# The first output projection of a two-block network in three rounded passes: weights split by ScalarE and GpSimd, outputs head by head

## The chip, the cores and the metric

The kernel runs on one core of a Trainium2 chip. The metric is the device time of one execution in microseconds, as the median over runs. TensorE multiplies (PE in the profile), VectorE (DVE), ScalarE (ACT) and GpSimd (POOL) work on whole tiles, and SyncE (SP) issues the weight loads in one queue. Each engine runs its own instructions in order; between engines the order is kept by semaphores.

## What is computed

Two blocks follow each other. The change lies in the first: 512 tokens (256 of context, 256 latent) of width 1024 pass through a gated linear attention with four heads, each scanned in both directions. The outputs of the heads are normalised, multiplied by a gate and projected.

```python
def gla_mixer(h_ctx, h_lat, w_in, a_w1, a_w2, a_b, norm_g, w_out, with_ctx_out):
    proj = h @ w_in
    q, k, v, r = jnp.split(proj, ...)      # 4 heads: q, k of 128, v of 256 each
    for d in range(2):
        g = jax.nn.log_sigmoid((h @ a_w1[d]) @ a_w2[d] + a_b[d]) / GLA_GATE_NORM
        ...                                # scan of each head, both directions summed
    # rms_norm of the head's output, times silu(r), then  @ w_out   (1024 x 1024)

x = x + g1 * o
x = x + g2 * conv_ffn(modulate(x, norm2_g, sh2, s2), ...)
```

Behind it stand the feed-forward block, a neighbourhood attention with a second feed-forward block, and the second network: a long convolution, a second scan and 64 experts.

## The kernel before

**Products.** A float32 product (`mm` on float32 tiles) leaves two records on TensorE. Many projections of the kernel are done otherwise, in three passes over rounded operands: `split_mm` (lines 537 to 541) multiplies the rounded weights by the rounded input (line 539), the rounded weights by the input's rest (540), and the weights' rest by the rounded input (541). The rounded part is a copy into a tile of the rounded float type (ScalarE, `activation` with Copy, helper `A`, line 1273), the rest is the difference, written in place (VectorE, `w_rest`, line 1837, `h_rest`, line 1842).

**Weights.** All weights of the first network come as slabs of 2 MB, one after the other through SP's queue (line 421), into four ring places of 4096 columns. `first_block_slabs` writes out the place of each and the semaphore value that frees it. The late modulation rows (`ada_w`, 20 slabs) use the places 0, 1 and 2, the two slabs of this projection (`gla_w_out`) the places 2 and 0. The first feed-forward slab follows in place 1, free after the last modulation product, the second in place 3, free once the last head's gated output (which lives there as `g_r`) is transposed.

**The scan** goes over eight (head, direction) pairs `hd`, here called heads 0 to 7 of the scan; each two of them make one output head. For each of them TensorE runs `scan_scores`, `scan_keys`, `gate_logits(hd + 2)`, `scan_updates` in two parts, with `late_turn` and, for odd ones from 3 on, `y_turn` (transposes of an output head, line 740) between, then `late_rows` (products of modulation rows, line 593) and for odd ones `scan_out` (lines 727 and 731). VectorE runs `decayed(hd + 1)` (lines 1979 and 1981, which wait for ScalarE's exponentials), `mask_scores`, `gated` for even ones, `states` (lines 2015 and 2018) and `cumulate(hd + 2)` (up to line 1969). ScalarE runs `keys_turned`, `late_read`, `gate_log(hd + 2)`, `y_turned` for odd ones from 3 on (it writes the transposed output with its gain into `g_qk`), `decays(hd + 2)` (seven exponentials) and `scan_norm` for odd ones. GpSimd has two multiplications in each (line 469).

**The projection** makes eight outputs `m` of 128 x 512, each from eight products `k`; `k` = 6 and 7 need the last output head. The first five outputs run ahead over `k` = 0 to 5 (line 765), with `late_turn(7)` after output 0 and `y_turn(3)` after output 2. Then the loop over `m` finishes them and makes the other three (line 777). After output `m`, `residual_norm` issues the norm product of output `m - 1` (line 524), which waits for ScalarE's square, which waits for VectorE's residual (line 1821). ScalarE and VectorE split the first two half slabs of the feed-forward block before the first of these residuals. When all squares are summed, the norm's factor, the modulation and `ffn(0, ...)` follow.

Of the kernel before, what the change touches and what calls it, by code (L numbers as in the profile page):

```python
# [83 lines left out]
def first_block_slabs():  # L84
# [23 lines left out]
    def ffn(l):  # L108
        for j in range(FC // 2):
            add("ffn_w_in", l, j, DC, 512, ("ffn_in_mm", 44 * l + 4 * j + 4), slot(), ("gla_y_tr", HEADS) if l == 0 and j == 1 else None)  # L110
        for m in range(DC):
            add("ffn_w_out", l, m, FC, P, ("ffn_out_mm", 8 * l + m + 1), slot())
# [13 lines left out]
def build(nc, d, out):  # L126
    ctx = ExitStack()
    with ctx:
# [85 lines left out]
        ada_late_sb = carve(g_aw1_at)(3, P)  # L214
        g_r = ring[3][:, :].rearrange("p (t n) -> p t n", n=D)
        g_kdt = kg[:, 0:4 * P].rearrange("p (a b) -> p a b", b=P)

# [101 lines left out]
        def slot(n):  # L319
            return ring[n][:, :]  # L320
# [138 lines left out]
        def _(pool):  # L459
# [5 lines left out]
            for hd in range(8):  # L465
                h, p = hd // 2, hd % 2
                for i, (x, y) in enumerate(((g_e3[:, two(h, p), :], g_qk[:, h, :]), (g_tm[:, p, :], g_qk[:, 4 + h, :]))):
                    pool.wait_ge(S["decay"], 7 * hd + 5 + i)
                    pool.tensor_tensor(x, x, y, ALU.mult).then_inc(S["late_decayed"], 1)

            pool.wait_ge(S["ffn_out_mm"], DC)
# [40 lines left out]
        def _(pe):  # L512
# [230 lines left out]
            for hd in range(8):  # L743
                scan_scores(hd)
                scan_keys(hd)
                if hd == 0:
                    pe.wait_ge(S["gla_r_ev"], 8)
                if hd + 2 < 8:
                    gate_logits(hd + 2)
                scan_updates(hd, 0)  # L750
                if hd >= 1:
                    late_turn(hd - 1)
                else:
                    late_rows(hd, 0)
                if hd >= 3 and hd % 2:
                    y_turn(hd // 2 - 1)
                scan_updates(hd, 1)
                for i in range(0 if hd else 1, ADA_BATCH[hd]):
                    late_rows(hd, i)
                if hd % 2:  # L760
                    scan_out(hd // 2)
            for m in range(GLA_AHEAD):
                w = got(FIRST["gla_out"] + m // 4)
                for k in range(6):
                    mm(pb[m][:, :], w[:, k, 128 * (m % 4):128 * (m % 4) + 128], g_qk[:, 4 * (k % 2) + k // 2, :], start=k == 0, stop=False,  # L765
                       skip_group_check=True)
                if m == 0:
                    late_turn(7)
                if m == 2:
                    y_turn(HEADS - 1)  # L770
            pe.wait_ge(S["gla_y_ev"], 2 * HEADS)
            for m in range(DC):
                w = got(FIRST["gla_out"] + m // 4)
                if m >= GLA_AHEAD:
                    pe.wait_ge(S["proj_x"], 2 * (m - GLA_AHEAD + 1))
                for k in range(6 if m < GLA_AHEAD else 0, DC):
                    last = mm(pb[m % GLA_AHEAD][:, :], w[:, k, 128 * (m % 4):128 * (m % 4) + 128], g_qk[:, 4 * (k % 2) + k // 2, :], start=k == 0, stop=k == DC - 1,  # L777
                              skip_group_check=True)
                last.then_inc(S["proj_mm"], 1)
                residual_norm("n2_0", m, TT)  # L780
# [32 lines left out]
            def na_out(j):  # L813
                pe.wait_ge(S["na_pt"], 2 * j + 2)
                if j >= 2:
                    pe.wait_ge(S["na_o_ev"], j - 1)
                for k in range(4):
# [35 lines left out]
            na_out(NA_H - 1)  # L853
            pe.wait_ge(S["na_o_ev"], NA_H)
            project("na_out", lambda k: n_o[:, k, :], NT, 2 * DC, 1, "n2_1")
# [403 lines left out]
        def _(act):  # L1259
# [236 lines left out]
            def y_turned(h):  # L1496
                act.wait_ge(S["gla_y_tr"], h + 1)
                for e in range(2):
                    A(g_qk[:, 4 * e + h, :], pb[6 + e][:, :], ACT.Copy, scale=col("gng", e)).then_inc(S["gla_y_ev"], 1)

            def r_read(s):
                for u in range(4):
# [10 lines left out]
            for hd in range(8):  # L1513
# [7 lines left out]
                if hd + 2 < 8:  # L1521
                    decays(hd + 2)
                if hd % 2:
                    scan_norm(hd // 2)
            late_read(7)
            y_turned(HEADS - 1)
            act.wait_ge(S["ada_late"], 8)
            for i in range(2):
                ffn_w_in_hi(0, i)
            squares("n2_0", DC, lambda c: xT[:, c, :], ("proj_x", 0, 2))  # L1530
            root_factor("n2_0", DC, 7, TT)
# [255 lines left out]
        def _(dve):  # L1787
# [233 lines left out]
            def gated(h):  # L2021
                dve.wait_ge(S["gla_r_ev"], 8)
                dve.wait_ge(S["o_ev"], 6 * h + 6)
                for tt in range(4):
                    y, o = g_r[:, tt, 256 * h:256 * h + 256], 256 * (tt % 2)
                    STT(out=y, in0=pb[6 + tt // 2][:, o:o + 256], scalar=g_n[:, 4 * (h % 2) + tt:4 * (h % 2) + tt + 1], in1=y, op0=ALU.mult, op1=ALU.mult)\
                        .then_inc(S["gate_y"], 1)

            def sine_argument(i):

# [19 lines left out]
            for hd in range(8):  # L2050
# [6 lines left out]
                if hd + 2 < 8:  # L2057
                    cumulate(hd + 2)
            late_columns(7)
            gated(HEADS - 1)  # L2060
            dve.wait_ge(S["ada_late"], 8)
            ada_gain(0, 1)
            for w in range(2):
                last = ada_gain(1, w)
            last.then_inc(S["mod_ready"], 1)
            for i in range(2):
                ffn_w_in_lo(0, i)
            for m in range(DC):
                residual(m, "proj_mm", "proj_x", m % GLA_AHEAD, TT, 0, 2)
            norm_mod("n2_0", 1, TT)  # L2070
            ffn(0, TT)
# [583 lines left out]
```

## Time and profile before

| | |
|---|---|
| median of three runs | 2468.7 us (2468.6 to 2469.37) |
| the profiled execution | 2463.28 us |
| its span | 2461.5 us |
| granted TensorE clock, mean | 0.919 |
| busy: PE, DVE, ACT, POOL | 2011.6, 909.3, 659.1, 58.4 us |
| TensorE on the chain that ended last | 52% of the span |
| transfers on that chain | 28% of the span |

The page gives each engine's busy time and divides the span into 40 slices with the busy share of each engine in tenths, the clock that TensorE was granted and what the transfers moved. The chain of waits goes back from the last instruction to what released it, step by step. The groups of instructions carry a line number; a line can be a helper's, as 1273 is for all of ScalarE's activations. The timeline lists one engine's instructions in order of time, runs of equal ones merged, with the idle time before them in brackets and the engine that ended it.

### The profile page before, as it was taken

Reading aid. Unit: us, or ns where it says so; the run is one execution under the profiler, and the core shown is the slowest. Engines: PE = TensorE matmul, PEld = TensorE weight load, DVE = VectorE, ACT = ScalarE, POOL = GpSimd, SP = SyncE. Lnnn points to the kernel's source line nnn. Section 1 sums busy time; section 2 is a strip of 40 time slices with the busy share of each in tenths; the row PEclk is TensorE's granted clock in tenths of the full one; section 3 lists DMA queues with packets and bytes.
Section 4 is the critical chain, followed back from the end, with each engine's and each line's share of the span. In section 5 each row is a group of like instructions: output and inputs, shape, how many; then the busy total and the mean of one; then the engine's idle time right before and its main releaser. Section 6 shows DMA issues by size and latency. Waiting matters only on the chain.

```text
span 2461.5 us, 37332 instructions
## 1 busy us (share of the span) xinstructions
PE 2011.6 (82%) x16358; PEld 1478.3 (60%) x16358; DVE 909.3 (37%) x1620; ACT 659.1 (27%) x1143; POOL 58.4 (2%) x83
## 2 busy tenths in 40 slices
PE   6998898999998998999999997766656666666665
PEld 3896555888776885899898454443333333333332
DVE  2345623434523328466475453322211111111112
ACT  4233414323413326454444301111111111111111
POOL 0010100000000001000010000000000000000000
PEclk8998999999999999999999998888888888888888
DMA  8106841222223231343540153999999999999996
GB/s 330 69 35 249 367 172 69 103 103 82 71 92 125 103 117 47 137 174 140 192 174 9 42 221 137 428 426 427 427 427 427 426 427 427 427 428 426 427 428 292
DMA packets 44544, 592.60 MB, mean 241 GB/s; under 512 B 5549, under 2 KB 5737, under 8 KB 8288
## 3 DMA queue, kind: packets, MB, share of 16 engines
q1 hardware_dynamic: 40608, 579.36, 57.5%
q0 software_dynamic: 2992, 8.96, 1.1%
q8 instruction: 130, 2.13, 0.4%
q10 hardware_dynamic: 784, 1.91, 0.2%
q14 instruction: 30, 0.25, 0.0%
HBM read 589.16 MB, written 1.05 MB: 240 GB/s over the span
## 4 chain that ended last, share of the span: by engine, by line
PE 52%; DMA 28%; DVE 6%; ACT 3%; issue 2%; SPq 0%; DVEq 0%; ACTq 0%
DMA s_ring<-in_w_up 12%; PE bank L539 10%; PE bank L541 10%; PE bank L540 10%; DMA s_arena<-in_w_up 8%; PE bank L1152 5%; DMA s_xT<-in_w_up 4%; DMA s_hT<-in_w_up 3%; PE bank L1166 2%; PE bank L593 1%; PE bank L777 1%; PE bank L582 1%; PE bank L1139 1%; DMA s_ring<-in_slabs 1%; PE bank L765 1%
## 5 line engine op out<-in xcount | busy, mean ns | idle before, releaser
L539 PE MATMUL bank<-s_arena_r 128*128 128x256 f32 (+2 forms) x1656 | 549.6, 332 | 39.3 <-DVE s_hT_r L1842 33.5
L1273 ACT ACTIVATE s_arena<-bank 32x256 f32<-32x256 f32 (+7 forms) x439 | 174.0, 409 | 1079.5 <-PE bank L1152 572.1
L541 PE MATMUL bank<-s_arena_r,s_ring_r 128*128 128x512 f32 (+2 forms) x1312 | 443.9, 338 | 0.0
L1152 PE MATMUL bank<-s_ring,s_arena 128*32 128x256 f32 x2048 | 297.6, 507 | 144.4 <-DMA s_xT<-in_w_up 47.4
L540 PE MATMUL bank<-s_hT_r,s_arena_r 128*128 128x512 f32 (+2 forms) x1096 | 369.8, 337 | 0.0
L539 PEld LDWEIGHTS bank<-s_arena_r 128*128 128x128 f32 x1656 | 315.3, 190 | 79.6 <-issue 37.9
L1837 DVE TENSOR_TENSOR s_ring_r<-s_ring,s_arena_r 128x2048 fp32r<-128x2048 f32 (+1 forms) x96 | 232.4, 2425 | 289.6 <-ACT s_arena_r L1273 289.5
L1152 PEld LDWEIGHTS bank<-s_ring,s_arena 128*32 128x32 f32 x2048 | 145.1, 144 | 220.9 <-issue 207.5
L541 PEld LDWEIGHTS bank<-s_arena_r,s_ring_r 128*128 128x128 f32 x1312 | 252.2, 192 | 27.2
L1273 ACT ACTIVATE s_arena_r<-s_ring 128x2048 fp32r<-128x2048 f32 (+1 forms) x96 | 193.2, 2016 | 138.1 <-PE bank L541 137.3
L2420 DVE TENSOR_TENSOR s_arena<-s_arena,bank 64x256 f32<-64x256 f32 x64 | 27.1, 423 | 543.9 <-ACT s_arena L1273 543.9
L540 PEld LDWEIGHTS bank<-s_hT_r,s_arena_r 128*128 128x128 f32 x1096 | 211.1, 193 | 21.8
L1152 PE MATMUL bank<-s_arena 128*32 128x256 f32 x1024 | 121.0, 489 | 75.5 <-DMA s_arena<-in_w_up 32.3
L1152 PEld LDWEIGHTS bank<-s_arena 128*32 128x32 f32 x1024 | 62.5, 139 | 113.3 <-issue 105.2
L540 PE MATMUL bank<-s_ring_r,s_arena_r 128*128 128x256 f32 (+1 forms) x464 | 130.1, 280 | 0.0
L1273 ACT ACTIVATE s_arena<-s_arena 128x512 f32<-128x512 f32 (+8 forms) x172 | 85.4, 532 | 160.6 <-DVE s_arena L1830 83.6
L1152 PE MATMUL bank<-s_xT,s_arena 128*32 128x256 f32 x512 | 92.8, 542 | 38.7 <-DMA s_ring<-in_w_up 38.7
L540 PE MATMUL bank<-s_arena_r 128*128 128x512 f32 (+1 forms) x352 | 120.0, 341 | 0.0
L2476 DVE COPY s_arena<-bank 32x256 f32<-32x256 f32 x128 | 54.3, 424 | 143.4 <-PE bank L1166 141.0
L1152 PE MATMUL bank<-s_hT,s_arena 128*32 128x256 f32 x512 | 82.2, 492 | 17.5 <-DMA s_ring<-in_w_up 17.5
L541 PE MATMUL bank<-s_arena_r,s_hT_r 128*128 128x256 f32 (+1 forms) x336 | 94.3, 281 | 0.0
L540 PEld LDWEIGHTS bank<-s_ring_r,s_arena_r 128*128 128x128 f32 (+1 forms) x464 | 85.9, 185 | 0.5
(332 smaller groups left out, 2621.9 us busy)
## 6 DMA issues: line engine op xcount, KB each, us to landing
s_ring<-in_slabs SPq DMA_DIRECT2D x72, 2048.0 KB, 8.2
s_ring<-in_w_down SPq DMA_DIRECT2D x32, 2048.0 KB, 28.9
s_ring<-in_w_up SPq DMA_DIRECT2D x32, 2048.0 KB, 32.9
s_ring<-in_w_gate SPq DMA_DIRECT2D x32, 2048.0 KB, 33.4
s_arena<-in_w_gate SPq DMA_DIRECT2D x16, 2048.0 KB, 33.5
s_arena<-in_w_up SPq DMA_DIRECT2D x16, 2048.0 KB, 34.0
s_arena<-in_w_down SPq DMA_DIRECT2D x16, 2048.0 KB, 28.9
s_ring<-in_slabs SPq DMA_DIRECT2D x16, 1408.0 KB, 6.4
```

The source lines that it names most:

```text
L539: mm(out, w_hi_, x_hi_, start=start, stop=False)
L540: mm(out, w_hi_, x_lo_, start=False, stop=False)
L541: return mm(out, w_lo_, x_hi_, start=False, stop=stop)
L582: last = mm(pb[m % 4][:, 0:T], w[:, c, 128 * (m % 4):128 * (m % 4) + 128], src(c), start=c == 0, stop=c == DC - 1)
L593: last = mm(bank[32 * j:32 * j + 32, o:o + P], ada_sc[:, c, :], w[:, c, P * j:P * j + P], start=c == 0, stop=c == DC - 1, skip_group_check ...
L765: mm(pb[m][:, :], w[:, k, 128 * (m % 4):128 * (m % 4) + 128], g_qk[:, 4 * (k % 2) + k // 2, :], start=k == 0, stop=False, skip_group_check ...
L1152: last = mm(pb[b][32 * q:32 * q + 32, 0:256], x[:, c, :], w[q // 2][:, c, 256 * (q % 2):256 * (q % 2) + 256], start=c == 0, stop=c == DC - ...
L1166: last = mm(pb[3 + b][32 * q:32 * q + 32, 0:256], e_hT[:, b, 64 * a + 32 * half_:64 * a + 32 * half_ + 32], w[:, 2 * half_ + a, 256 * q:25 ...
L1273: return act.activation(out, in_, func, **kw)
L1837: TTn(view_r, view, hi.bitcast(F32), ALU.subtract).then_inc(S["w_lo"], 1)
L2420: return TTn(e_hid[0:64, b, :], e_sg[0:64, b, :], pb[b][64:128, 0:256], ALU.mult)
L2476: dve.tensor_copy(y_g[32 * j:32 * j + 32, g % 2, 256 * q:256 * q + 256], pb[3 + b][32 * q:32 * q + 32, 0:256]).then_inc(S["y_dve"], 1)
```

## The change

The products of the projection are done by `split_mm`. Their rounded weights (`g_wo_hi`) take the place of the ring's place 1 for outputs 0 to 3 and of the scan's states `g_S` for outputs 4 to 7. ScalarE makes them in four halves (`wo_rounded`): two in the scan's last step, once the last modulation product is done, two behind `late_read(7)`. GpSimd subtracts them from the weights in place. The gated output of each head is rounded by ScalarE (`y_hi`, into the place of that head's values `g_v`) and its rest formed by VectorE (`y_rest`, in place): heads 0 and 1 in the steps 4 and 6 of the scan, behind `decays` and `cumulate`, head 2 at its end, head 3 behind its gain. A wait on each `k` replaces the one wait for the last head. The first feed-forward slab is free only after four outputs, and its two splits move behind the squares and residuals of outputs 3 and 4. The semaphore `na_o_ev` gets an offset for its later users, `rope_s`, `gla_r_ev` and `late_decayed` are counted on.

```diff
@@ first_block_slabs: ffn
-            add("ffn_w_in", ..., slot(), ("gla_y_tr", HEADS) if l == 0 and j == 1 else None)
+            add("ffn_w_in", ..., slot(), {0: ("proj_mm", 4), 1: ("gla_y_tr", HEADS)}.get(j) if l == 0 else None)
@@ tiles
+        g_y_lo = arena_r[:, 0:8 * TT].rearrange("p (a b) -> p a b", b=TT)
+        g_y_hi = arena_r[:, 8 * TT:8 * TT + 4 * D].rearrange("p (t n) -> p t n", n=D)
+        g_wo_hi = [x.rearrange("p (c n) -> p c n", n=512) for x in (ring_r[1][:, :], arena_r[:, g_S_at:g_S_at + 4096])]
+        A_YO_HI, A_WO_HI, A_WO_LO, A_YO_LO = 8, 8, 16, 8
@@ GpSimd, behind the scan's multiplications
+            for q in range(4):
+                n = FIRST["gla_out"] + q // 2
+                pool.wait_ge(S["gla_r_ev"], A_WO_HI + q + 1)
+                pool.tensor_tensor(half(place_r[n], q % 2), half(place[n], q % 2), half(g_wo_hi[q // 2], q % 2).bitcast(F32), ALU.subtract)\
+                    .then_inc(S["late_decayed"], 1)
@@ TensorE
+            def gla_out(m, first, last_k):
+                wh, wl, o = g_wo_hi[m // 4], place_r[FIRST["gla_out"] + m // 4], 128 * (m % 4)
+                if m % 2 == 0:
+                    pe.wait_ge(S["late_decayed"], A_WO_LO + m // 2 + 1)
+                for k in range(first, last_k):
+                    h, e = k // 2, k % 2
+                    pe.wait_ge(S["rope_s"], A_YO_LO + k + 1)
+                    last = split_mm(pb[m % GLA_AHEAD][:, :], wh[:, k, o:o + 128], wl[:, k, o:o + 128], g_y_hi[:, :, 256 * h + P * e:256 * h + P * e + P],
+                                    g_y_lo[:, 4 * e + h, :], k == 0, k == DC - 1)
+                return last
             for m in range(GLA_AHEAD):
-                w = got(FIRST["gla_out"] + m // 4)
-                for k in range(6):
-                    mm(pb[m][:, :], w[:, k, ...], g_qk[:, 4 * (k % 2) + k // 2, :], start=k == 0, stop=False, skip_group_check=True)
+                gla_out(m, 0, 6)
...
-            pe.wait_ge(S["gla_y_ev"], 2 * HEADS)
             for m in range(DC):
-                w = got(FIRST["gla_out"] + m // 4)
                 if m >= GLA_AHEAD:
                     pe.wait_ge(S["proj_x"], 2 * (m - GLA_AHEAD + 1))
-                for k in range(6 if m < GLA_AHEAD else 0, DC):
-                    last = mm(...)
-                last.then_inc(S["proj_mm"], 1)
+                gla_out(m, 6 if m < GLA_AHEAD else 0, DC).then_inc(S["proj_mm"], 1)
                 residual_norm("n2_0", m, TT)
@@ ScalarE
+            def y_hi(h):
+                act.wait_ge(S["gla_y_ev"], 2 * h + 2)
+                for e in range(2):
+                    o = 256 * h + P * e
+                    A(g_y_hi[:, :, o:o + P], g_qk[:, 4 * e + h, :].rearrange("p (t n) -> p t n", n=P), ACT.Copy).then_inc(S["na_o_ev"], 1)
+
+            def wo_rounded(q):
+                n = FIRST["gla_out"] + q // 2
+                act.wait_ge(S[landed[n][0]], landed[n][1])
+                if q == 0:
+                    act.wait_ge(S["ada_mm"], 2 * ADA_N)
+                if q == 2:
+                    act.wait_ge(S["o_mm"], HEADS)
+                A(half(g_wo_hi[q // 2], q % 2), half(place[n], q % 2), ACT.Copy).then_inc(S["gla_r_ev"], 1)
@@ ScalarE, the scan's loop
                 if hd + 2 < 8:
                     decays(hd + 2)
+                if hd in (4, 6):
+                    y_hi(hd // 2 - 2)
+                if hd == 7:
+                    y_hi(2)
+                    for q in range(2):
+                        wo_rounded(q)
                 if hd % 2:
                     scan_norm(hd // 2)
             late_read(7)
+            for q in range(2, 4):
+                wo_rounded(q)
             y_turned(HEADS - 1)
+            y_hi(HEADS - 1)
             act.wait_ge(S["ada_late"], 8)
-            for i in range(2):
-                ffn_w_in_hi(0, i)
-            squares("n2_0", DC, lambda c: xT[:, c, :], ("proj_x", 0, 2))
+            for c in range(DC):
+                square(norms["n2_0"][0], c, xT[:, c, :], ("proj_x", 0, 2))
+                if c in (3, 4):
+                    ffn_w_in_hi(0, c - 3)
@@ VectorE
+            def y_rest(h):
+                for e in range(2):
+                    o = 256 * h + P * e
+                    dve.wait_ge(S["na_o_ev"], 2 * h + e + 1)
+                    TTn(g_y_lo[:, 4 * e + h, :]..., g_qk[:, 4 * e + h, :]..., g_y_hi[:, :, o:o + P].bitcast(F32), ALU.subtract).then_inc(S["rope_s"], 1)
@@ VectorE, the scan's loop
                 states(hd)
                 if hd + 2 < 8:
                     cumulate(hd + 2)
+                if hd in (4, 6):
+                    y_rest(hd // 2 - 2)
+            y_rest(2)
             late_columns(7)
             gated(HEADS - 1)
+            y_rest(HEADS - 1)
...
-            for i in range(2):
-                ffn_w_in_lo(0, i)
             for m in range(DC):
                 residual(m, "proj_mm", "proj_x", m % GLA_AHEAD, TT, 0, 2)
+                if m in (3, 4):
+                    ffn_w_in_lo(0, m - 3)
```

## Rows read from the trace of the kernel before

**Rows 1.** Page, 40 slices of the span: busy tenths of TensorE, GB/s moved

```profile
PE   6998898999998998999999997766656666666665
...
GB/s 330 69 35 249 367 172 69 103 103 82 71 92 125 103 117 47 137 174 140 192 174 9 42 221 137 428 426 427 427 427 427 426 427 427 427 428 426 427 428 292
```

**Rows 2.** Chain of waits, scan's head 5 and projection: start us, us, what

```profile
282.92 11.81 DMA s_ring<-in_slabs
...
294.77 1.95 PE bank L593 x64
...
387.75 6.88 PE bank L777 x16
```

**Rows 3.** Lines 765 and 777, TensorE: count, duration ns min/median/max, first and last start

```profile
L765 PE MATMUL bank<-s_arena,s_ring x60: 592/592/697, 333.0 to 359.5; 128*128 128x512 f32 x60
...
L777 PE MATMUL bank<-s_arena,s_ring x68: 592/592/592, 359.9 to 394.0; 128*128 128x512 f32 x68
```

**Rows 4.** Timeline, TensorE, 345 to 440: start us, us, line, count, [idle before]

```profile
359.95 3.60 PE L777 MATMUL bank<-s_arena,s_ring 128*128 128x512 f32 x8
...
396.25 1.13 PE L524 MATMUL bank<-s_sq,s_ones 128*128 128x512 f32 x2 [0.77 <-ACT s_sq L1273]
404.72 0.76 PE L539 MATMUL bank<-s_arena_r 128*128 128x512 f32 x1 [7.35 <-DVE s_hT_r L1842]
...
406.14 0.63 PE L539 MATMUL bank<-s_arena_r 128*128 128x512 f32 x1
...
407.42 0.63 PE L539 MATMUL bank<-s_arena_r 128*128 128x512 f32 x1
```

**Rows 5.** Line 539, TensorE, 413 to 439.9 us, columns as in rows 3

```profile
L539 PE MATMUL bank<-s_arena_r x39: 389/397/398, 412.8 to 439.4; 128*128 128x512 f32 x39
```

**Rows 6.** Timeline, TensorE, end of the scan

```profile
291.44 1.13 PE L717 MATMUL bank<-s_arena 64*128 64x256 f32 x6 [0.79 <-DVE s_arena L2018]
...
310.36 5.37 PE L593 MATMUL bank<-s_ring,s_arena 128*32 128x128 f32 x128
...
322.80 3.70 PE L593 MATMUL bank<-s_ring,s_arena 128*32 128x128 f32 x128
```

**Rows 7.** Timelines of ScalarE and VectorE, one split each; line 469, GpSimd

```profile
411.68 1.90 ACT L1273 ACTIVATE s_arena_r<-s_ring 128x2048 fp32r<-128x2048 f32 x1
...
413.61 2.29 DVE L1837 TENSOR_TENSOR s_ring_r<-s_ring,s_arena_r 128x2048 fp32r<-128x2048 f32 x1 [1.03 <-ACT s_arena_r L1273]
...
L469 POOL TENSOR_TENSOR s_arena<-s_arena x16: 1264/1399/1863, 165.9 to 304.1; 128x512 f32<-128x512 f32 x16
```

**Rows 8.** Line 421, slab loads: 366 to 372 us, then 0 to 12 us

```profile
L421 SPq DMA_DIRECT2D s_ring<-in_slabs x1: 328/328/328, 368.9 to 368.9; - x1
...
DMA to landing us min/median/max: 7.9/7.9/7.9
...
L421 SPq DMA_DIRECT2D s_ring<-in_slabs x4: 417/541/762, 1.2 to 2.9; - x4
...
DMA to landing us min/median/max: 13.7/22.0/29.8
```

**Rows 9.** Timelines of VectorE and ScalarE, one residual and one square

```profile
363.58 0.88 DVE L1821 SCALAR_TENSOR_TENSOR s_xT<-bank,s_mod,s_xT 128x256 f32<-128x256 f32 x2 [0.84 <-PE bank L777]
...
364.49 0.63 ACT L1273 ACTIVATE s_sq<-s_xT 128x512 f32<-128x512 f32 x1 [1.09 <-DVE s_xT L1821]
```

**Rows 10.** Two stretches: us, each engine's busy time, granted clock, DMA share, GB/s

```profile
310.00:315.00 5.00, 5.00 (x112) 4.66 (x113) 1.45 (x3) 0.00 (x0) 0.00 (x0) 0.66 0.19 39
405.00:410.00 5.00, 5.00 (x13) 3.89 (x13) 2.48 (x5) 5.00 (x11) 0.00 (x0) 0.52 0.02 3
```

**Rows 11.** Timelines of ScalarE and VectorE, heads 4 and 5 of the scan

```profile
284.72 2.91 ACT L1273 ACTIVATE s_arena<-s_arena 128x512 f32<-128x512 f32 x7 [9.32 <-DVE s_arena L1969]
...
285.38 1.29 DVE L1981 TENSOR_TENSOR s_arena<-s_arena 128x512 f32<-128x512 f32 x2 [0.69 <-ACT s_arena L1273]
...
289.87 1.51 DVE L2018 SCALAR_TENSOR_TENSOR s_arena<-s_arena,bank 128x256 f32<-128x256 f32 x3
```

More of the change, by code:

```diff
@@ L109, in ffn @@
         for j in range(FC // 2):
-            add("ffn_w_in", l, j, DC, 512, ("ffn_in_mm", 44 * l + 4 * j + 4), slot(), ("gla_y_tr", HEADS) if l == 0 and j == 1 else None)
+            add("ffn_w_in", l, j, DC, 512, ("ffn_in_mm", 44 * l + 4 * j + 4), slot(), {0: ("proj_mm", 4), 1: ("gla_y_tr", HEADS)}.get(j) if l == 0 else None)
         for m in range(DC):
@@ L761, in _ @@
                     scan_out(hd // 2)
+            def gla_out(m, first, last_k):
[8 more added lines that the diff above has]
+                return last
             for m in range(GLA_AHEAD):
-                w = got(FIRST["gla_out"] + m // 4)
-                for k in range(6):
-                    mm(pb[m][:, :], w[:, k, 128 * (m % 4):128 * (m % 4) + 128], g_qk[:, 4 * (k % 2) + k // 2, :], start=k == 0, stop=False,
-                       skip_group_check=True)
+                gla_out(m, 0, 6)
                 if m == 0:
@@ L770, in _ @@
                     y_turn(HEADS - 1)
-            pe.wait_ge(S["gla_y_ev"], 2 * HEADS)
             for m in range(DC):
-                w = got(FIRST["gla_out"] + m // 4)
                 if m >= GLA_AHEAD:
                     pe.wait_ge(S["proj_x"], 2 * (m - GLA_AHEAD + 1))
-                for k in range(6 if m < GLA_AHEAD else 0, DC):
-                    last = mm(pb[m % GLA_AHEAD][:, :], w[:, k, 128 * (m % 4):128 * (m % 4) + 128], g_qk[:, 4 * (k % 2) + k // 2, :], start=k == 0, stop=k == DC - 1,
-                              skip_group_check=True)
-                last.then_inc(S["proj_mm"], 1)
+                gla_out(m, 6 if m < GLA_AHEAD else 0, DC).then_inc(S["proj_mm"], 1)
                 residual_norm("n2_0", m, TT)
@@ L815, in na_out @@
                 if j >= 2:
-                    pe.wait_ge(S["na_o_ev"], j - 1)
+                    pe.wait_ge(S["na_o_ev"], A_YO_HI + j - 1)
                 for k in range(4):
@@ L853, in _ @@
             na_out(NA_H - 1)
-            pe.wait_ge(S["na_o_ev"], NA_H)
+            pe.wait_ge(S["na_o_ev"], A_YO_HI + NA_H)
             project("na_out", lambda k: n_o[:, k, :], NT, 2 * DC, 1, "n2_1")
@@ L2027, in gated @@
                         .then_inc(S["gate_y"], 1)
+            def y_rest(h):
+                for e in range(2):
+                    o = 256 * h + P * e
+                    dve.wait_ge(S["na_o_ev"], 2 * h + e + 1)
+                    TTn(g_y_lo[:, 4 * e + h, :].rearrange("p (t n) -> p t n", n=P), g_qk[:, 4 * e + h, :].rearrange("p (t n) -> p t n", n=P),
+                        g_y_hi[:, :, o:o + P].bitcast(F32), ALU.subtract).then_inc(S["rope_s"], 1)
             def sine_argument(i):
```

## The prediction

> **What bounds the kernel now.** I read the page's slices first: TensorE is busy for nine or more tenths of most of the first half, and only then do transfers set the pace [rows 1]. The output projection lies between 333 and 396 us, so what the engines before the expert loads lose or gain there reaches the end one for one. The chain of waits comes next [rows 2]. It has two pieces that matter: in the scan's head 5 it runs over a weight transfer of the late modulation rows that lands at 294.73 us, with TensorE there only just before it, and over the projection it runs along TensorE's own products. Of the 71.7 us from the first product at 333.0 [rows 3] to the first product of the feed-forward block at 404.72 [rows 4] the products take 64 x 0.86 = 55.0: two records each, 128 records in all [rows 3], 16 records in 6.88 us [rows 2].
>
> **The passes.** A product in three rounded passes has a pace in this trace. 39 first passes of the feed-forward block start between 412.8 and 439.4 us at full clock, 38 steps of 0.70 us [rows 5]. 64 x 0.70 = 44.8, so the products fall by **10.2 us**. The moving operand of the new products is four pieces of 128 columns and no row here shows that shape; I price it like the contiguous one (0), with 0 to 0.03 us a product, 2 us in all, as the bound above, and nothing below, since 512 columns remain to be streamed.
>
> **The weights' split at its start.** Rounding of the first half slab on ScalarE waits for the last late rows, which end at 326.5 [rows 6]. The copy takes 1.9 us [rows 7], so GpSimd starts at 328.4. No GpSimd operation of 2048 elements is in the trace; four times its multiplications of 512 elements (two inputs, like the subtraction) is 5.1 by the shortest, 5.6 by the median and 7.5 by the longest [rows 7]. VectorE is idle then, so I take the shortest: 333.5, against 333.0 at which TensorE is free. **+0.5 us**, with 0 and 2.9 as the ends. The other three halves are done by about 348.6; outputs 2, 4 and 6 want them at 342, 351 and 366 at the earliest, so they are hidden, and remain so at 7.5 us each. The copies on ScalarE lie in its idle time and do not delay the last head's square sums, as the first two end at 330.3, before the scan's last products at 333.0.
>
> The Trainium skill, GPSIMD Engine Reference, section 3.1, gives 4.5 us for a two-input operation of 2048 float32 elements, and its section 4.1 advises VectorE for such work. By the 4.5 the split would end at 332.9 and the 0.5 us would be nothing; the estimate from the rows is 5.1, and no row shows the length itself. The advice speaks against the change, but costs little here because the other three splits are covered.
>
> **The last output head.** Transposes, gain, rounding and rest of output head 3 now have 3 outputs x 6 x 0.70 us ahead of the turn and two outputs (8.4 us) behind it; two gains and two roundings on ScalarE at 0.63 and two rests on VectorE at about 0.65 [rows 9, 11], about 4 us, end before that. Nothing is added.
>
> **The first feed-forward slab.** This is the step that gives back most. Its ring place now holds the rounded weights of outputs 0 to 3, so its load waits for the fourth output, and it stands in the SP queue ahead of the loads of slabs 1 and 2, which start behind it; they land by about 381, and their first split is wanted only when the feed-forward block runs, so that costs nothing. In the times of the trace before (the scan's own shift left out): start 333.5, 30 products 21.0, the transposes in between 1.1 (before, 25.8 of products and as much of transposes lay between 333.0 and 359.95), so 355.6. Eight products 5.6, two norm products of two 0.43 us records each 1.7 [rows 2], a wait of 0.3 for the first square: the fourth output ends at 363.2. A slab of this size lands 7.9 us after its issue with an empty queue [rows 8]: 371.1. ScalarE rounds half of it, 1.9: 373.0. VectorE forms the rest, 2.3 [rows 7]: 375.3. Only behind this, in VectorE's order, comes the residual of output 4, 0.87, and then its square on ScalarE, 0.63 [rows 9]: 376.9. TensorE has output 4, two norm products and output 5 to do meanwhile, 1.4 + 1.7 + 5.6, and stands at the norm product of output 4 at 371.9. It waits **5.0 us**. The second half slab (hi 1.9, lo 2.3) delays output 5's residual, which is ready at 382.5 while TensorE arrives at 383.4: hidden, with 0.9 to spare. Then 3 norm products, 11.2 of products and 0.9 for the last square: 391.6 where 396.25 stood [rows 4]. The 8.5 us to the feed-forward block do not change. So the projection itself gains 10.2 - 0.5 - 5.0 = 4.7 us.
>
> **The clock.** After the idle time of 7.35 us ahead of the feed-forward block the granted clock is 0.52 of full, its lower level of 1.2 GHz, from 405 to 410 [rows 10], and a product takes 1.28 us instead of 0.70 [rows 4]. The new wait of 5.0 us is nearest to that one. Four products at 1.28 cost 4 x 0.58 = **+2.3 us**; 0 and 4.6 are the ends.
>
> **The scan.** The roundings of output heads 0 to 2 are put between the scan's steps. In scan head 4 ScalarE rounds output head 0 only behind the seven decay exponentials of scan head 6, 284.72 to 287.63; VectorE's new rests come ahead of its decayed products of scan head 6, and wait for that rounding. Today those products start 0.7 us behind the first exponential, at 285.38 [rows 11]. With the change: roundings at 287.53 to 288.7 (0.63 each), the rests (0.65 each) end at 289.4, and the decayed products start there instead of at 285.38. Masks and states follow; 0.3 us of a wait on the way is absorbed, so the states that stand at 289.87 come 3.7 us later. TensorE's second half of the state updates waits for those states already, 0.79 us before 291.44 [rows 6]; behind it stand the late rows of scan head 5. They have their transfer at 294.73 [rows 2], which hides 0.3. So **+3.4 us** goes to the end of the scan. The ends are 0 and 4.1. The same pair in scan heads 6 and 7 lies in idle time: no decays follow, and all of VectorE's steps then wait for TensorE. TensorE's wait before these updates grows from 0.79 to about 4.2 us; in scan head 6 a wait of 1.78 us at the same place is followed by a clock of 0.66 [rows 10], and 128 late row products took 5.37 where they take 3.70 at full clock [rows 6]. **+1.7 us**, between 0 and 3.4.
>
> **The sum.** -10.2 + 0.5 + 5.0 + 2.3 + 3.4 + 1.7 = +2.7 us. The profiled execution took 2463.28 us for a span of 2461.5, so it would take 2466.0; the median of the runs is 2468.7, 5.4 above the profiled one, and becomes 2471.4.
>
> **Rivals.** A difference of 0.2% (4.9 us) is about what a measurement of this kernel can tell from no change.
> *The gain comes through.* If the scan's wait is absorbed (its late rows are bound by transfers in head 5) and the clock holds, 4.7 us are left: 2464.0, still no visible change. If the slab were also in time, that is, with no TensorE wait at output 4, it would be 9.7: 2459.0. The first half is spoken against by the small spare time of 0.3 us at the transfer, the second by the order residual behind rest. 0.10 for the first, 0.09 for the second.
> *Slower: three loads share.* The first slab's load is issued together with those of slabs 1 and 2. If the engines interleave them, all three land together, after 3 x 2.1 MB at 428 GB/s [rows 1], 14.7, and about 3 of latency, 17.6 instead of 7.9 us, and TensorE waits 9.7 more: 2481.1. It decides as soon as the first of three lands beyond about 10 us, for 2.2 us more than the sum is 2473.6. Against it: of four slabs issued at the start behind another load, the first landed after 13.7 and the last after 29.8 us [rows 8], in order. 0.07.
> The Trainium skill, DMA: Bandwidth & Descriptors, section "Queues, rings and completion order", says that each engine consumes a ring's descriptors in order; by that rule the loads do not share, the time is that of the sum, and those landings agree.
> *Slower: clock and GpSimd at their upper ends.* 2.3 + 1.7 + 2.4 more: 2477.8. Shorter forms of it begin at 2474. 0.14.
> *The forecast*, within 2467.4 (no clock loss) and 2474: 0.60.
>
> **How the numbers follow.** 8 in 10 need the forecast, the first half of the first rival and the clock rival: 2464 to 2478. Faster by over 0.2% is below 2463.8: 0.09 and 0.03 of its neighbour at 2464, 0.12. Slower is above 2473.6: 0.07 + 0.14 and 0.05 from the upper edge of the forecast, 0.26. Within: 0.55 + 0.07 = 0.62.
>
> **What would show it.** Products of the projection 0.70 us apart; the first GpSimd subtraction about 5.1 us long, ending near TensorE's first product; one TensorE wait of some 5 us before the norm product of output 4, ended by ScalarE's square; VectorE idle some 3 to 4 us before the rests in head 4, and TensorE's state updates of head 5 waiting as long; a low clock behind both waits. If the projection's first product comes at its old time, the scan term is wrong; if no wait stands at output 4, the slab term is.

## The result and the profile after

The changed kernel takes 2472.3 us as the median of 20 runs (2466.67 to 2476.04), the kernel before 2468.31 us over the 20 runs beside it (2462.98 to 2471.02). The ratio, which takes in all the runs, is 1.0022 with a 95% interval of 1.0015 to 1.0029, that is 5.4 us more, between 3.7 and 7.2; the medians alone differ by 4.0. The forecast was 2471.4 us in a range of 2464 to 2478. The interval lies above 1, so the change is slower, if only by 0.2%.

The profiled execution of after took 2475.01 us. It lies near the slow end of its runs, the one of before (2463.28) near the fast end of its own, so the 11.7 us between their spans are more than the change. Up to the feed-forward block the two traces differ by 6.4 us (411.08 against 404.72 in [rows 4]); the other 5.3 appear far behind the change, and the difference of the runs does not show them.

From the page of after, whose busy time of TensorE is that of before to the tenth: the span, the busy times, and GpSimd's slices, of which the sixth now holds the weights' split.

```profile
span 2473.2 us, 37490 instructions
...
PE 2011.6 (81%) x16422; PEld 1494.1 (60%) x16422; DVE 915.0 (37%) x1628; ACT 672.1 (27%) x1155; POOL 76.6 (3%) x87
...
POOL 0010130000000001000010000000000000000000
```

The chain of waits of after, 280 to 415 us (start us, us, engine, what it was on). It answers to [rows 2].

```profile
287.13 0.62 ACT s_arena_r L1287
...
288.43 1.75 DVE s_arena_r L2074
...
295.35 2.07 PE bank L727 x6
...
323.87 11.22 DMA s_ring<-in_slabs
335.11 1.92 ACT s_ring_r L1287
337.10 4.53 POOL s_ring_r L478
...
371.80 7.79 DMA s_ring<-in_slabs
379.62 1.92 ACT s_arena_r L1287
381.56 2.29 DVE s_ring_r L1878
383.86 0.80 DVE s_xT L1862 x2
384.68 0.64 ACT s_sq L1287
385.36 2.08 PE bank L534 x2
```

Before, the chain ran over a transfer in scan head 5. Here it runs over ScalarE's rounding at 287.13 and VectorE's rests behind it, then VectorE's decayed products, to the updates on TensorE at 295.35; then over the landing of the first slab of the projection's weights at 335.11, its rounding and GpSimd's subtraction; then over the landing of the first feed-forward slab at 379.59, its rounding, its rest, the residual and the square of output 4, to the norm product at 385.36. These are the three places that the prediction named, but at the second it had the last late rows and not the landing ahead of the rounding.

TensorE's timeline in the scan, the two parts of the updates of scan head 5 and one second part with the late rows in scan head 6 (start us, us, line, count, idle before). They answer to [rows 6].

```profile
288.80 1.13 PE L727 MATMUL bank<-s_arena 64*128 64x256 f32 x8 [0.68 <-ACT s_arena L1287]
...
295.35 2.07 PE L727 MATMUL bank<-s_arena 64*128 64x256 f32 x6 [4.07 <-DVE s_arena L2059]
...
317.88 5.93 PE L603 MATMUL bank<-s_ring,s_arena 128*32 128x128 f32 x128
```

The wait before the second part grew from 0.79 to 4.07 us. The late rows at 317.88 took 5.93 where they take 3.70 at full clock.

ScalarE's seven exponentials in scan head 4, VectorE's rests and decayed products behind them and its next rests in scan head 6, and GpSimd's multiplications beside the first (timelines).

```profile
284.32 2.91 ACT L1287 ACTIVATE s_arena<-s_arena 128x512 f32<-128x512 f32 x7 [8.54 <-DVE s_arena L2010]
...
287.78 2.40 DVE L2074 TENSOR_TENSOR s_arena_r<-s_arena,s_arena_r 128x512 fp32r<-128x512 f32 x2 [3.49 <-ACT s_arena_r L1287]
290.10 1.28 DVE L2022 TENSOR_TENSOR s_arena<-s_arena 128x512 f32<-128x512 f32 x2
...
319.42 1.29 DVE L2074 TENSOR_TENSOR s_arena_r<-s_arena,s_arena_r 128x512 fp32r<-128x512 f32 x2
...
286.68 2.95 POOL L473 TENSOR_TENSOR s_arena<-s_arena 128x512 f32<-128x512 f32 x2 [19.33 <-ACT s_arena L1287]
```

VectorE waited 3.49 us for the rounding, and its decayed products, at 285.38 in [rows 11], start at 290.10. The two rests took 2.40 us beside GpSimd's work and 1.29 without it.

TensorE's timeline in the projection, answering to [rows 4] and [rows 5]. The first three rows are first passes with the second and third passes between them left out, then the norm product of output 4, two first passes behind it and the first product of the feed-forward block.

```profile
341.67 0.50 PE L549 MATMUL bank<-s_arena_r,s_ring_r 128*128 128x512 f32 x1 [0.54 <-POOL s_ring_r L478]
...
342.47 0.39 PE L549 MATMUL bank<-s_arena_r,s_ring_r 128*128 128x512 f32 x1
...
343.18 0.40 PE L549 MATMUL bank<-s_arena_r,s_ring_r 128*128 128x512 f32 x1
...
385.36 2.08 PE L534 MATMUL bank<-s_sq,s_ones 128*128 128x512 f32 x2 [4.93 <-ACT s_sq L1287]
...
388.51 0.63 PE L549 MATMUL bank<-s_arena_r 128*128 128x512 f32 x1
...
389.79 0.63 PE L549 MATMUL bank<-s_arena_r 128*128 128x512 f32 x1
...
411.08 0.77 PE L549 MATMUL bank<-s_arena_r 128*128 128x512 f32 x1 [7.35 <-DVE s_hT_r L1883]
```

A product takes 0.71 us in its three passes (342.47 to 343.18), as elsewhere in the kernel ([rows 5]: 0.70). Behind the wait of 4.93 us a product takes 1.28 us (388.51 to 389.79); the granted clock from 387 to 390 us is 0.50, the engine's lower level of 1.2 GHz.

GpSimd's subtractions of the first weights slab (count, ns min/median/max, first and last start), and SP's loads issued between 370 and 374 us with their time to landing (min/median/max).

```profile
L478 POOL TENSOR_TENSOR s_ring_r<-s_ring,s_ring_r x2: 4520/4571/4622, 337.1 to 341.6; 128x2048 fp32r<-128x2048 f32 x2
```

```profile
L425 SPq DMA_DIRECT2D s_ring<-in_slabs x3: 328/430/432, 371.8 to 372.6; - x3
...
DMA to landing us min/median/max: 7.8/12.3/16.7
```

The three loads that stand at the fourth output land after 7.8, 12.3 and 16.7 us, one behind the other. The first is not slowed by the two behind it.

### The profile page after: what moved, and what is told of

The parts are those of the page before. It is cut to its first block, busy times and chain, and to the rows that moved or that the text cites. A ratio compares the mean times of both kernels' runs of the same rounds, so it can differ in the third digit from the quotient of the medians.

```text
span 2473.2 us, 37490 instructions
## 1 busy us (share of the span) xinstructions
PE 2011.6 (81%) x16422; PEld 1494.1 (60%) x16422; DVE 915.0 (37%) x1628; ACT 672.1 (27%) x1155; POOL 76.6 (3%) x87
## 4 chain that ended last, share of the span: by engine, by line
PE 49%; DMA 28%; DVE 6%; ACT 3%; issue 3%; POOL 0%; SPq 0%; DVEq 0%; ACTq 0%
DMA s_ring<-in_w_up 12%; PE bank L549 10%; PE bank L551 10%; PE bank L550 10%; DMA s_arena<-in_w_up 8%; PE bank L1166 5%; DMA s_xT<-in_w_up 4%; DMA s_hT<-in_w_up 3%; PE bank L1180 2%; PE bank L592 1%; PE bank L1153 1%; ACT s_arena_r L1287 1%; PE bank L534 1%; PE bank L993 1%; PE bank L1186 1%
## 5 line engine op out<-in xcount | busy, mean ns | idle before, releaser
L549 PE MATMUL bank<-s_arena_r 128*128 128x256 f32 (+2 forms) x1688 | 564.9, 335 | 39.7 <-DVE s_hT_r L1883 33.0
L551 PE MATMUL bank<-s_arena_r,s_ring_r 128*128 128x512 f32 (+2 forms) x1376 | 470.0, 342 | 0.0
L549 PEld LDWEIGHTS bank<-s_arena_r 128*128 128x128 f32 x1688 | 322.3, 191 | 83.0 <-issue 38.7
L551 PEld LDWEIGHTS bank<-s_arena_r,s_ring_r 128*128 128x128 f32 x1376 | 264.9, 192 | 30.0
L550 PE MATMUL bank<-s_arena_r 128*128 128x512 f32 (+1 forms) x384 | 132.7, 346 | 0.0
L1166 PE MATMUL bank<-s_hT,s_arena 128*32 128x256 f32 x512 | 77.2, 468 | 17.8 <-DMA s_ring<-in_w_up 17.8
```

The source lines that it names most:

```text
L549: mm(out, w_hi_, x_hi_, start=start, stop=False)
L550: mm(out, w_hi_, x_lo_, start=False, stop=False)
L551: return mm(out, w_lo_, x_hi_, start=False, stop=stop)
L1166: last = mm(pb[b][32 * q:32 * q + 32, 0:256], x[:, c, :], w[q // 2][:, c, 256 * (q % 2):256 * (q % 2) + 256], start=c == 0, stop=c == DC - ...
```

## The experiments

The table gives, from one profiled execution of each kernel, TensorE's wait before the second part of the updates in scan head 5, the start of the projection's first product, the start of the last norm product and the time between these two; then the ratio of the runs to runs of the kernel before taken beside them, with its 95% interval. Differences between two kernels are taken between such ratios. The start of the first product also holds what happened ahead of the change, which differs between executions: order_only has the scan of the kernel before, and its first product comes 2.8 us later. In two_passes, whose scan is that of the change, TensorE waits 1.48 us before the first part of these updates, where the change shows 0.68, and so less before the second.

| kernel | wait in scan | first product | last norm product | between | ratio to before |
|---|---|---|---|---|---|
| before | 0.79 | 333.00 | 396.25 | 63.3 | 1 |
| the change | 4.07 | 341.67 | 402.61 | 60.9 | 1.0022 (1.0015 to 1.0029) |
| scan_later | none | 333.11 | 394.02 | 60.9 | 0.9992 (0.9983 to 1.0000) |
| split_later | 4.07 | 334.92 | 388.11 | 53.2 | 0.9993 (0.9983 to 1.0002) |
| both_later | 0.28 | 335.42 | 388.62 | 53.2 | 0.9959 (0.9945 to 0.9972) |
| order_only | 0.79 | 335.84 | 404.35 | 68.5 | 1.0016 (1.0006 to 1.0025) |
| rest_later | none | 336.90 | 396.72 | 59.8 | 1.0002 (0.9993 to 1.0012) |
| two_passes | 2.93 | 340.11 | 389.05 | 48.9 | 0.9973 (0.9962 to 0.9984) |
| both_vector | none | 334.54 | 387.70 | 53.2 | 0.9956 (0.9942 to 0.9969) |

### Undoing the order in the scan: scan_later

```diff
-                if hd in (4, 6):
-                    y_hi(hd // 2 - 2)
+                if hd == 6:
+                    y_hi(0)
+                    y_hi(1)
```

and the same for `y_rest` on VectorE.

> The changed kernel, with the rounding and the rest of output head 0 moved from scan head 4 to scan head 6, ahead of those of output head 1; nothing else is moved. Theory 1 (VectorE's rests wait behind the seven exponentials and hold up the states, for which TensorE waits): the wait of TensorE before the second part of the state updates of scan head 5 falls from 4.07 us to about 0.8 us, the low clock behind it goes too, the scan ends 4 to 8 us earlier than 341.1 us, near 333 to 337, and the kernel takes 4 to 8 us less than the changed one (about 2464 to 2468 us). Theory 2 (the end of the scan is set by the transfers of the modulation slabs): the wait moves to the late rows, on a transfer, and under 1.5 us are won.

ScalarE's seven exponentials in scan head 4; TensorE's timeline: both parts of the updates in scan head 5 and the late rows behind them, second part and late rows in scan head 6, norm product of output 4.

```profile
282.11 2.91 ACT L1287 ACTIVATE s_arena<-s_arena 128x512 f32<-128x512 f32 x7 [8.54 <-DVE s_arena L2011]
...
285.55 1.13 PE L727 MATMUL bank<-s_arena 64*128 64x256 f32 x8 [1.31 <-ACT s_arena L1287]
...
289.11 1.60 PE L727 MATMUL bank<-s_arena 64*128 64x256 f32 x6
290.64 3.70 PE L603 MATMUL bank<-s_ring,s_arena 128*32 128x128 f32 x128
...
307.25 2.07 PE L727 MATMUL bank<-s_arena 64*128 64x256 f32 x6 [1.78 <-DVE s_arena L2060]
309.25 6.00 PE L603 MATMUL bank<-s_ring,s_arena 128*32 128x128 f32 x128
...
376.70 2.08 PE L534 MATMUL bank<-s_sq,s_ones 128*128 128x512 f32 x2 [4.83 <-ACT s_sq L1287]
```

No wait stands before the updates at 289.11, and the late rows behind them run at full clock, 3.70 us. (In this execution a short low clock lay ahead of them and drew out the work before, so that even the old 0.79 us of wait is filled; in both_later 0.28 us of it are seen.) So the low clock behind the second part is gone, but not that of scan head 6, where the updates take 2.07 and the late rows 6.00 us as in the change. The first product starts at 333.11, 8.6 us earlier than in the changed kernel; 2.2 us of this lie ahead of the moved steps (the exponentials start at 282.11 against 284.32), 6.4 behind them. The wait at output 4 is untouched, 4.83 us. The runs give 0.9992 against 1.0022, 7.4 us less. Theory 1 holds; no wait on a transfer took the place of the one that went.

### Undoing the order at the slab: split_later

```diff
-                if c in (3, 4):
-                    ffn_w_in_hi(0, c - 3)
+                if c in (5, 6):
+                    ffn_w_in_hi(0, c - 5)
```

and the same for `ffn_w_in_lo` on VectorE.

> The changed kernel, with the two splits of the first feed-forward slab behind the squares and residuals of outputs 5 and 6 instead of 3 and 4; the load is still issued after the fourth output. Theory 1 (TensorE waits at the norm product of output 4 because its residual stands behind a rest that waits for the slab): this wait of 4.93 us goes, the slab has landed by the time it is asked for, and its splits (1.9 + 2.3 us) fit between two outputs of 6.5 us; the kernel takes 5 to 8 us less than the changed one (about 2464 to 2467 us), the upper part of it from the clock. Theory 2 (the wait only moves on): a wait of 2 us or more appears at the norm product of output 6 or 7, or ahead of the feed-forward block, and under 3 us are won.

TensorE's timeline: second parts of the updates with the late rows in scan heads 5 and 6, and the last norm product; the next wait of over 0.4 us after the first product is the one at the last norm product.

```profile
292.96 1.79 PE L727 MATMUL bank<-s_arena 64*128 64x256 f32 x6 [4.07 <-DVE s_arena L2059]
294.68 4.66 PE L603 MATMUL bank<-s_ring,s_arena 128*32 128x128 f32 x128
...
311.91 1.13 PE L727 MATMUL bank<-s_arena 64*128 64x256 f32 x6 [1.77 <-DVE s_arena L2059]
312.97 3.70 PE L603 MATMUL bank<-s_ring,s_arena 128*32 128x128 f32 x128
...
388.11 1.13 PE L534 MATMUL bank<-s_sq,s_ones 128*128 128x512 f32 x2 [0.77 <-ACT s_sq L1287]
```

Two stretches of this kernel and of the changed one (us, busy times of PE, PEld, DVE, ACT and POOL, granted clock, DMA share, GB/s), first split_later, then the change.

```profile
379.00:387.00 8.00, 8.00 (x33) 5.85 (x31) 4.02 (x6) 2.43 (x2) 0.00 (x0) 1.00 0.30 129
```

```profile
379.00:387.00 8.00, 3.07 (x10) 1.66 (x8) 3.08 (x3) 4.24 (x3) 0.00 (x0) 0.81 1.00 430
387.00:395.00 8.00, 8.00 (x28) 6.07 (x26) 3.47 (x4) 0.73 (x2) 0.00 (x0) 0.76 0.16 66
```

TensorE is busy through 379 to 387 at a clock of 1.00. In the changed kernel it is busy for 3.07 us of these eight, and the clock is 0.81 and then 0.76. The projection takes 53.2 instead of 60.9 us, 7.7 less: 4.9 of wait and 2.8 of clock. The runs give 7.2 us less (0.9993 against 1.0022). The load is issued no earlier here; only who stands behind the splits changed. Theory 1 holds.

The scan of this kernel is that of the change, with the same wait of 4.07 us. But its updates at 292.96 took 1.79 us where those of the change took 2.07, and the late rows 4.66 where those of the change took 5.95. From the start of the second part to the step behind the late rows a scan head takes 4.7 us at full clock. In scan head 5 the low clock added 3.2 us to this in the change and 1.6 here, behind the same wait of 4.07 us.

Scan head 6 must be kept apart. All nine kernels wait 1.77 or 1.78 us there before the second part. Behind this wait the low clock added 3.2 us in the change, but as much in scan_later and 2.9 in order_only, which have no long wait in scan head 5; it added 1.6 to 1.7 in before, both_later, rest_later and both_vector, and nothing here and in two_passes, which have the long wait. So the 3.2 us of scan head 6 in the trace of the change cannot be put down to the wait in scan head 5.

### Both orders undone: both_later

> Both moves together on the changed kernel. Theory 1 (the two waits and their clock are all that was given back): the sum of the two, 9 to 16 us less than the changed kernel, 2457 to 2463 us, that is 5 to 11 us below the kernel before, of which 10.2 us are the faster products. Theory 2 (the faster products are lost for another reason as well): no faster than the kernel before by more than 3 us.

TensorE's timeline: second part of the updates in scan head 5, first product.

```profile
293.50 1.13 PE L727 MATMUL bank<-s_arena 64*128 64x256 f32 x6 [0.28 <-DVE s_arena L2060]
...
335.42 0.50 PE L549 MATMUL bank<-s_arena_r,s_ring_r 128*128 128x512 f32 x1 [0.50 <-POOL s_ring_r L478]
```

The median is 2455.86 us and the ratio 0.9959: 10.1 us faster than before (6.9 to 13.6) and 15.5 below the change, against 14.6 for the two moves added up. That is what the faster products give when nothing is handed back, 10.2 us less the 0.5 that TensorE waits for GpSimd. In the traces the projection takes 10.1 us less from its first product on (53.2 against 63.3); the first product itself comes 2.4 us later than in the trace of before, but so it does, by 2.8 us, in order_only with the scan of before. Theory 1 holds. This kernel is faster than both.

### The order alone on the kernel before: order_only

The edit is the change's new free value of the first feed-forward slab and its places of the splits, and nothing else of it.

> The kernel before, float32 products, with only the change's new order of the first feed-forward slab: its load waits for the fourth output, its splits stand behind the squares and residuals of outputs 3 and 4. Theory 1 (the slab's chain of 7.9 + 1.9 + 2.3 + 0.87 + 0.63 us from the fourth output on sets the norm product of output 4): the slower products cover more of it, 0.86 x 10 products and two norm products from the fourth output on, so TensorE waits about 3.4 us there instead of 4.93 us, and the kernel is 3 to 6 us slower than before with the clock. Theory 2 (the wait belongs to the rounded products and not to the order): no wait there and no difference from before.

TensorE's timeline: norm product of output 4.

```profile
385.43 2.08 PE L524 MATMUL bank<-s_sq,s_ones 128*128 128x512 f32 x2 [3.37 <-ACT s_sq L1273]
```

The wait is 3.37 us, where the chain counted from the fourth output gave 3.4: the slower float32 products cover more of the same chain. The ratio is 1.0016, 3.9 us slower (1.5 to 6.2). The wait belongs to the order, not to the rounded products. Theory 1 holds.

### Which engine's order costs in the scan: rest_later

Only `y_rest(0)` moves to scan head 6; `y_hi(0)` stays in scan head 4.

> The changed kernel, with only VectorE's rest of output head 0 moved from scan head 4 to scan head 6; ScalarE's rounding stays in scan head 4. Theory 1 (VectorE's order is what costs: its decayed products, masks and states stand behind the rest): the wait of 4.07 us before the second part of the updates of scan head 5 falls to 1.5 us or less, what is left being the 1.1 us by which ScalarE's rounding moves the copy of the turned keys; the kernel takes 3 to 7 us less than the changed one, nearly what moving both gives. Theory 2 (ScalarE's 1.1 us in a full stretch is the larger part): the wait before the first part of those updates grows by over 1 us or that before the second stays over 2.5 us, and under 2 us are won.

ScalarE's seven exponentials in scan head 4; TensorE's timeline: the two parts of the updates in scan head 5, then the norm product of output 4.

```profile
285.89 2.91 ACT L1287 ACTIVATE s_arena<-s_arena 128x512 f32<-128x512 f32 x7 [9.31 <-DVE s_arena L2010]
...
290.37 1.13 PE L727 MATMUL bank<-s_arena 64*128 64x256 f32 x8 [1.49 <-ACT s_arena L1287]
...
293.93 1.61 PE L727 MATMUL bank<-s_arena 64*128 64x256 f32 x6
...
380.51 2.08 PE L534 MATMUL bank<-s_sq,s_ones 128*128 128x512 f32 x2 [4.85 <-ACT s_sq L1287]
```

The wait before the second part is gone. The wait before the first part is 1.49 us, close to the 1.31 of scan_later, where ScalarE's rounding is gone as well; but a wait also depends on when TensorE comes. Counted from the start of the exponentials, the first part starts after 3.44 us in before and in scan_later (282.11 to 285.55), and after 4.48 here (285.89 to 290.37) and in the change (284.32 to 288.80). So ScalarE's rounding, 1.13 us long, does move the first part, by 1.0 us. The runs give 4.9 us less than the change (1.0002 against 1.0022), and scan_later 7.4 less; their intervals overlap (0.9993 to 1.0012 and 0.9983 to 1.0000). So most of the cost is VectorE's order. What ScalarE's 1.0 us costs in the end, from nothing to some 2 us, is left open by these runs.

### Less work for TensorE, same waits: two_passes

The middle pass, rounded weights times the rest of the outputs, is left out, so the result lacks that part.

> The changed kernel, with the middle pass (rounded weights times the rest of the input) left out of every product of this projection, 64 matmuls of 0.23 us or 14.9 us of TensorE work less; all waits and splits stay. Theory 1 (the slab's chain, counted from the fourth output, sets the norm product of output 4): the 10 products between the fourth output and that norm product shrink by 2.3 us without effect, the wait grows from 4.93 to about 7.2 us, and the kernel takes about 12.6 us less than the changed one (2459 to 2461 us). Theory 2 (TensorE's work is the bound throughout, the wait is a fixed delay): the wait stays near 4.9 us and all 14.9 us or more are won.

TensorE's timeline: norm product of output 4.

```profile
375.47 2.08 PE L534 MATMUL bank<-s_sq,s_ones 128*128 128x512 f32 x2 [7.10 <-ACT s_sq L1288]
```

The wait grew from 4.93 to 7.10 us as the ten products ahead of it shrank. The runs give 12.1 us less than the change (0.9973 against 1.0022), of 14.9 us less work. Theory 1 holds: the norm product of output 4 comes at a time that the fourth output and the slab set, not TensorE's work between.

### The weights' rest on VectorE: both_vector

```diff
+            y_rest(2)
+            for q in range(2):
+                n = FIRST["gla_out"] + q // 2
+                dve.wait_ge(S["gla_r_ev"], A_WO_HI + q + 1)
+                TTn(half(place_r[n], q % 2), half(place[n], q % 2), half(g_wo_hi[q // 2], q % 2).bitcast(F32), ALU.subtract).then_inc(S["wo_lo"], 1)
```

on both_later, with GpSimd left two of the four.

> The kernel with both moves, with the rests of the first two half slabs of weights formed by VectorE instead of GpSimd. Theory 1 (VectorE is idle there and takes 2.3 us for what took GpSimd 4.5 to 4.6): the wait of 0.50 us before the first product goes, unless the landing of the slab sets it, nothing else changes, and the kernel is within 1.5 us of the one with both moves, 2454 to 2458 us. Theory 2 (VectorE's waits for the splits delay the last head's gated output or the late columns): TensorE waits ahead of a late product, and the kernel is over 2 us slower than with both moves.

Timelines of ScalarE (the two roundings), VectorE (the two rests) and TensorE (end of the scan, first product).

```profile
329.00 3.71 ACT L1289 ACTIVATE s_ring_r<-s_ring 128x2048 fp32r<-128x2048 f32 x2 [4.13 <-DMA s_ring<-in_slabs]
...
330.94 4.49 DVE L2117 TENSOR_TENSOR s_ring_r<-s_ring,s_ring_r 128x2048 fp32r<-128x2048 f32 x2 [3.76 <-ACT s_ring_r L1289]
...
333.54 1.08 PE L741 MATMUL bank<-s_arena 128*64 128x256 f32 x6
334.54 0.50 PE L549 MATMUL bank<-s_arena_r,s_ring_r 128*128 128x512 f32 x1
```

VectorE needs 4.49 us for two where GpSimd needs 4.52 or more for each. The first product follows the scan without idle time, and no new wait stands ahead of a late product, as theory 1 said. The ratio is 0.9956 against 0.9959; half a microsecond is below what the runs can tell.

## Why the prediction was right, and where its terms were off

**Products, -10.2 us.** Right. The pace was 0.70 us as priced, four pieces of 128 columns cost nothing, and both_later shows the whole of it in the runs.

**The slab, +5.0 us.** Right in place, cause and size: 4.93 us, ended by ScalarE's square; the chain is that of the prediction, step by step. The landing took 7.8 us where 7.9 were taken from [rows 8]. Two experiments move it as the chain says, to 3.37 with slower and 7.10 with fewer passes. The rival of three loads that share the engines fell with the landings of 7.8, 12.3 and 16.7 us. By the Trainium skill, DMA: Bandwidth & Descriptors, "Queues, rings and completion order", a ring's descriptors are taken in order, and these landings agree.

**GpSimd, +0.5 us.** The sum was right, 0.54, by luck: two errors cancel. The subtraction took 4.52 to 4.63 us and not 5.1: four times the shortest operation of 512 elements in [rows 7] is too much; if a part of it is fixed, the scaling counted that part four times, which no run here shows by itself. The Trainium skill, GPSIMD Engine Reference, section 3.1, has 4.5 us for an addition of two inputs of that size, and here the page was nearer than my estimate from rows. But ScalarE's rounding started 0.6 us after the last late rows (335.11 against 334.51 in the trace of after), on the landing of the weights slab, and not on those rows as I had it. I had not looked at when that slab lands: with another load ahead it took 11.2 us. In split_later and rest_later the same wait was 0.92 and 1.16 us.

**The clock at the slab, +2.3 us.** Measured 2.8 us: the products cost the 1.6 us of eight passes at 0.43 instead of 0.23, and the norm product 2.08 where two records take 0.86. The second was missing in my count. Behind the same place it was 2.9 us in scan_later and 1.8 in rest_later, and 1.9 in order_only.

**The scan, +3.4 us of wait.** Right in place and cause: 0.79 grew to 4.07 us, 3.3 more, and rest_later shows that VectorE's order makes it. The parts were less exact. The two rests took 2.40 us, not the 1.3 priced, with GpSimd at work beside them; the steps behind them absorbed 0.8 us and not 0.3; and the prediction had nothing for ScalarE's rounding moving the first part by 1.0 us. Counted from the exponentials, the states come 4.3 us later (9.47 against 5.15), not 3.7.

**The clock in the scan, +1.7 us.** This is the term that was mis-sized, for the profiled execution at least. From the first part of the updates of scan head 5 to the first product the change takes 52.9 us (288.80 to 341.67), and the kernel before 44.8 (288.16 to 333.00). Of the 8.0 more, 3.3 are the wait and 0.5 GpSimd, and 0.5 of a wait for a transfer in scan head 5 of before are no longer seen, so some 4.7 are left for the clock: 3.2 in scan head 5, and in scan head 6 3.2 where before has 1.7. In split_later, with the same wait, the stretch is 48.5 us (286.41 to 334.92); it has 1.6 us of low clock in scan head 5 and none in scan head 6, as much in all as before. The price of 1.7 was read in scan head 6 of the kernel before, and at that very place the nine traces have 0 to 3.2. Behind the long wait itself it was 3.2 and 1.6, within the ends of 0 and 3.4 that the prediction gave.

**The sum.** The forecast was 9.7 us of net gain and 12.4 handed back, +2.7. The runs show 10.1 gained (both_later against before) and 15.5 handed back (both_later against the change), +5.4. The gain was right; the part handed back came out 3.1 us larger, of which 0.5 is the clock at the slab (2.8 against 2.3), and the clock in the scan may be the rest. The runs point that way: against the change the move in the scan is worth 7.4 us and the one at the slab 7.2, each on top of the other 8.4 and 8.1, where the forecast had 5.1 and 7.3. But the intervals of the runs are as wide as these differences, so it is not shown. That 2471.4 came within 1 us of the median of 2472.3 is partly luck, as the change came out at twice the forecast of +2.7.

## What to carry to other kernels

A step put into an in-order engine's queue costs by what stands behind it and by what it waits for, not by its length alone: two short rests on VectorE cost about 5 us, since they waited for ScalarE and the scan's products waited for them, and a split of 4.2 us cost 7.7 in the trace because it waited for a landing and one residual stood behind it. When a buffer's last use moves later, count from that use to the landing, the splits and whatever is queued behind them, and place the splits at the first point where that count is over; here two outputs later made all the difference. Before a change that seems to bring nothing is dropped, look for whether its gain is handed back at one or two such places: the same faster products were worth +5.4 us or -10.1 us.

## What the runs showed of the hardware

Two waits of 4.07 us in the same place of the same code were followed by 3.2 us of low clock in one execution and by 1.6 in another, waits of 4.8 to 4.9 us at the slab by 1.8 to 2.9, and one wait of 1.78 us that all nine kernels have by anything from 0 to 3.2. The low clock behind a wait should be carried as a range, and one trace does not give its price. Two rests of 512 elements on VectorE took 2.40 us while GpSimd multiplied two tiles of the same size, and 1.29 us in scan head 6 without it; in the kernel before, a multiplication of this size on VectorE took 1.00 us beside GpSimd (at 288.02) and 0.69 without it (at 318.00). The Trainium skill, GPSIMD Engine Reference, section 1, says that the two engines share their way to the on-chip memory and that VectorE's instructions with two inputs from it contend; this trace agrees. Executions of one kernel on a single core spread by 9.4 us here (2466.67 to 2476.04), more than the change moved; a pair of traces shows where a difference arises but not how large the change is.
